# Two matmuls per slice in place of three: x's low and high halves side by side in one 512-column operand, and the two bank halves joined by ScalarE and VectorE

## The chip, the cores and the metric

The kernel runs on one core of a Trainium2 chip. The metric is the device time of one execution in microseconds (us). The kernel before takes 1995.85 us, the median of three runs (1995.22, 1995.85 and 1999.67).

## The reference

Two layers of an encoder trunk work on x of 256 tokens x 2048 channels, all in float32. Each layer does this:

```
h = RMSNorm(x)
u, s5_gate, z, xbc, dt, q, k, v, att_gate, merge_logits = split(h @ w_in)
y_s5  = S5(u) -> GELU -> GLU (a 1024x1024 product) -> * silu(s5_gate)
y_ssd = Mamba-2 SSD(z, xbc, dt), then a gated RMSNorm
y_att = sliding-window attention(q, k, v) * silu(att_gate)
merged = sum over the three branches of sigmoid(merge_logits_b) * (y_b @ w_branch_b)
x = x + merged @ w_out
```

Nearly all arithmetic is in the four weight products: `h @ w_in` (2048 x 11,792 columns), the GLU, the three branch products and `merged @ w_out` (2048 x 2048).

## The kernel before

**Exact products from two halves.** Weights arrive from DRAM as a stream of 1 MB slices (`raw`, 128 x 2048 float32, four buffers). ScalarE rounds a slice to its high part (`hi`, line 683, writes `w_hi`), VectorE subtracts to get the low part (`lo`, line 971, writes `w_lo` over `raw`), and TensorE forms three products: high weights with low x, low weights with high x, and high with high. x has the same two parts, `h_hi` and `h_lo`.

**Two shapes of slice.** A *feature-major* slice ("pair", line 1565) holds 128 output features for all 2048 inputs. The weights are the stationary operand, and the 256 tokens stream. For each of 16 steps k, `prod3` issues three matmuls of 256 columns into one half of a PSUM bank, 48 matmuls in all. A *token-major* slice ("block", line 1590) holds 512 output features; x is stationary, and 512 columns of weights stream.

**The stages of a layer**, with the numbers of slices:
- *Front*: 16 slices. n = 0 to 3 are B and C of the SSD, 4 and 5 are k, 6 and 7 are v (written out, not a pair), 8 to 15 are u. Between them VectorE and ScalarE run long chains of small operations (S5 parameters, dt, convolutions, the norm of k), and TensorE has a few small products that wait for them: `k_ss` (line 1667), `k_rot` (line 1677).
- *Inner*: a loop of 4 x 8 feature-major slices, with one S5 tile in each turn: TensorE's `kv` after slice 1 (lines 1692 and 1698), `cs` after slice 5 (lines 1708 and 1714), VectorE's S5 work at slices 2, 3 and 4.
- *Gates*: a loop of 4 x 12 token-major slices, with S5, SSD and attention tiles.
- *Side gate and GLU*: 8 feature-major slices, then 4 GLU slices ("units", two products of 256 columns side by side).
- *Branches*: 24 token-major slices. *Out*: 16 feature-major slices; x_new = product + x_old.

**What sets the order.** Every engine runs its own instruction list in order, written out by hand; semaphores couple them. `pair_done` counts finished slices. TensorE uses two banks of `mm` in turn, so slice n waits until the result of slice n-2 has been read. VectorE reads each result (`tt_(..., bank, rstd, mult)`, lines 1163 to 1176, 1309, 1459) and then does `lo` for slice n+3. ScalarE does `hi` for slice n+3 as soon as its data has landed; nothing in this list waits for TensorE. SyncE loads slice j+4 once slice j is finished; in the side-gate stage its list also holds two loads of `gin` that wait for VectorE's `ssd_w3` (line 452), and the load of the next weights stands behind them.

Of the kernel before, what the change touches and what calls it, by code (L numbers as in the profile page):

```python
# [15 lines left out]
P = 128  # L16
# [19 lines left out]
N_SG, N_GLU, N_BR, N_OUT, N_LAYER = 96, 104, 108, 132, 148  # L36
BRANCHES = (1, 2, 0)
# [100 lines left out]
def program(nc, x, norm_w, params, consts, bdense, stream, xs_out, order):  # L138

    with ExitStack() as ctx:  # L140
# [23 lines left out]
        h_hi = sb("h_hi", [P, KT, TOK], F32R)  # L164
        h_lo = sb("h_lo", [P, KT, TOK], F32R)
# [40 lines left out]
        ta = sb("ta", [P, TOK])  # L206
        kcur = sb("kcur", [P, TOK])
        vcur = sb("vcur", [P, 2, 64])
        gt = sb("gt", [P, 2, WIDE])
        tA = sb("tA", [P, TOK])  # L210
# [69 lines left out]
        in_read = sem("in_read")  # L280
        gate_sum = sem("gate_sum")
# [391 lines left out]
        def _(e):  # L673
# [19 lines left out]

            def inv_sqrt(S_, name, out, logs, v, wait):
# [12 lines left out]
            with e.Fori(0, DEPTH) as L:  # L707
# [8 lines left out]
                nb = start(L, 0)  # L716
                for n in range(16):
                    hi(nb, n + LEAD)
# [53 lines left out]
                with e.Fori(0, 4) as I:  # L772
                    nb = start(L, N_IN, I, 8)
                    W.s5(L, I, 0)
                    for s in range(8):
                        hi(nb, s + LEAD)
# [127 lines left out]

                for n in range(12):
                    hi(nb, n + LEAD)
# [58 lines left out]
        def _(e):  # L965
# [29 lines left out]
            S_A = {LV: LA, MV: MA}  # L995

# [8 lines left out]
            with e.Fori(0, DEPTH) as L:  # L1005
# [152 lines left out]
                nb = e.snap(L * N_LAYER)  # L1158
                for n in range(16):
# [3 lines left out]
                    e.wait_ge(pair_done, nb + (n + 3))  # L1163
                    bank = mm[:, n % 2, 0:256]
                    if n < 4:
                        LV.mark(tt_(proj[:, BC + n, :], bank, rstd[:], ALU.mult), f"in{n}")
                    elif n < 6:
                        LV.mark(tt_(kt[:, n - 4, :], bank, rstd[:], ALU.mult), "k_raw" if n == 5 else "in4")
# [4 lines left out]
                    elif 8 <= n < 14:  # L1173
                        LV.mark(tt_(by_lag(proj[:, U + n - 8, :]), by_chunk(bank), by_chunk(rstd[:]), ALU.mult), f"in{n}")
                    elif n >= 14:
                        tt_(by_lag(proj[:, U + n - 8, :]), by_chunk(bank), by_chunk(rstd[:]), ALU.mult).then_inc(in_read, 1)
# [126 lines left out]
                with e.Fori(0, 4) as I:  # L1303
                    nb = e.snap(L * N_LAYER + N_IN + I * 8)
                    W.s5(L, I, 0)
# [738 lines left out]
```

## Time and profile before

| | |
|---|---|
| median of 3 runs | 1995.85 us |
| the profiled execution | 1993.25 us, of which the span is 1991.5 us |
| mean granted TensorE clock | 0.99 |
| TensorE busy | 96% of the span |
| VectorE busy | 66% |
| ScalarE busy | 48% |
| GpSimd busy | 27% |
| DRAM traffic | 188 GB/s over the span |

The span is the stretch from the first to the last instruction of the profiled execution. A group of instructions is told by its line in the kernel. Matmuls overlap in the records (each is shown with its way through the array), so the time that one takes from the next is read from the distance of their starts, not from their durations.

### The profile page before, as it was taken

How to read it: one execution, taken by the hardware profiler on the slowest of the kernel's cores; microseconds unless marked ns; L12 is line 12 of the kernel's file. 1: busy time of each engine (PE TensorE's matmuls, PEld its weight loads, DVE VectorE, ACT ScalarE, POOL GpSimd, SP SyncE). 2: the span in 40 equal slices, each digit the busy share in tenths (PEclk: the TensorE clock that was granted, in tenths of full speed). 3: DMA queues.
4: the chain of work that ended last, by engine and by line, in shares of the span. 5: the costliest groups of instructions: out<-in, count | busy, mean ns of one | idle time of the engine just before them, and what ended most of it. 6: DMA issues, size and time to landing. Idle time of an engine off the chain costs nothing.

```text
span 1991.5 us, 38600 instructions
## 1 busy us (share of the span) xinstructions
PE 1911.2 (96%) x13680; PEld 1704.9 (86%) x13680; DVE 1311.9 (66%) x1729; ACT 946.8 (48%) x1160; POOL 530.2 (27%) x578
## 2 busy tenths in 40 slices
PE   4998999999999999999979799999999999999998
PEld 4898999877777798889978799997777778988898
DVE  6855666687776757665567556667776766576654
ACT  5233333566656645333343333336656665543333
POOL 4105444262442000002411254452442410000033
PEclk9998999999999999999989999999999999999999
DMA  6345555555454456665544545555554554566656
GB/s 256 141 154 201 182 181 183 178 182 177 168 177 158 158 180 233 243 233 200 202 155 145 196 165 182 183 187 175 175 170 164 174 171 169 177 244 236 233 194 206
DMA packets 79442, 372.78 MB, mean 187 GB/s; under 512 B 20560, under 2 KB 27216, under 8 KB 40528
## 3 DMA queue, kind: packets, MB, share of 16 engines
q1 hardware_dynamic: 76560, 359.99, 51.8%
q0 software_dynamic: 1088, 6.80, 0.8%
q10 hardware_dynamic: 1696, 4.72, 0.6%
q8 instruction: 58, 0.95, 0.2%
q14 instruction: 40, 0.33, 0.0%
HBM read 351.80 MB, written 21.76 MB: 188 GB/s over the span
## 4 chain that ended last, share of the span: by engine, by line
PE 83%; DVE 6%; issue 4%; DMA 2%; ACT 2%; POOL 1%; SPq 1%; DVEq 0%; ACTq 0%; POOLq 0%
PE mm L1602 13%; PE mm L1604 13%; PE mm L1603 13%; PE mm L1561 11%; PE mm L1562 11%; PE mm L1563 11%; DMA raw<-in_stream 2%; DVE w_lo L974 1%; ACT w_hi L687 1%; PE b L1698 1%; PE by L1762 1%; PE bs L1708 1%; PE b L1753 1%; PE bs L1714 1%; PE b L1774 1%
## 5 line engine op out<-in xcount | busy, mean ns | idle before, releaser
L687 ACT ACTIVATE w_hi<-raw 128x2048 fp32r<-128x2048 f32 x299 | 571.4, 1911 | 696.0 <-DMA raw<-in_stream 685.0
L974 DVE TENSOR_TENSOR w_lo<-raw,w_hi 128x2048 fp32r<-128x2048 f32 x299 | 690.4, 2309 | 245.7 <-ACT w_hi L687 236.8
L1561 PE MATMUL mm<-h_lo,w_hi 128*128 128x256 f32 x2240 | 644.5, 288 | 37.6 <-DVE h_lo L978 37.3
L1562 PE MATMUL mm<-h_hi,w_lo 128*128 128x256 f32 x2240 | 637.4, 285 | 0.0
L1563 PE MATMUL mm<-h_hi,w_hi 128*128 128x256 f32 x2240 | 637.2, 284 | 0.0
L1561 PEld LDWEIGHTS mm<-h_lo,w_hi 128*128 128x128 f32 x2240 | 433.9, 194 | 42.1 <-DVE h_lo L978 37.5
L1562 PEld LDWEIGHTS mm<-h_hi,w_lo 128*128 128x128 f32 x2240 | 433.8, 194 | 1.5 <-issue 1.0
L1563 PEld LDWEIGHTS mm<-h_hi,w_hi 128*128 128x128 f32 x2240 | 433.5, 194 | 0.0
L1602 PE MATMUL mm<-w_lo,h_hi 128*128 128x512 f32 x768 | 317.2, 413 | 0.0
L1604 PE MATMUL mm<-w_hi,h_lo 128*128 128x512 f32 x768 | 301.1, 392 | 0.0
L1603 PE MATMUL mm<-w_hi,h_hi 128*128 128x512 f32 x768 | 299.8, 390 | 0.0
L668 POOL TENSOR_TENSOR ssum<-ssum,proj 128x256 f32<-128x256 f32 x32 | 76.3, 2384 | 388.4 <-ACT proj L960 388.4
L1602 PEld LDWEIGHTS mm<-w_lo,h_hi 128*128 128x128 f32 x768 | 144.2, 188 | 38.2 <-issue 9.4
L1604 PEld LDWEIGHTS mm<-w_hi,h_lo 128*128 128x128 f32 x768 | 144.1, 188 | 32.1
L1603 PEld LDWEIGHTS mm<-w_hi,h_hi 128*128 128x128 f32 x768 | 144.5, 188 | 27.2
L1602 PE MATMUL mm<-w_lo,ys 128*128 128x512 f32 x384 | 150.2, 391 | 5.6 <-DVE acc L1512 5.6
L1604 PE MATMUL mm<-w_hi,ys 128*128 128x512 f32 x384 | 149.5, 389 | 0.0
L1603 PE MATMUL mm<-w_hi,ys 128*128 128x512 f32 x384 | 149.4, 389 | 0.0
L978 DVE TENSOR_TENSOR proj<-mm,rstd 128x256 f32 (+1 forms) x104 | 47.1, 453 | 142.5 <-PE mm L1563 142.1
L538 POOL TENSOR_TENSOR bw<-bd,lam 128x512 f32<-128x512 f32 x16 | 21.5, 1346 | 279.9 <-DMA lam<-lscr 279.9
L1602 PEld LDWEIGHTS mm<-w_lo,ys 128*128 128x128 f32 x384 | 72.1, 188 | 21.1 <-DVE acc L1512 6.5
L1604 PEld LDWEIGHTS mm<-w_hi,ys 128*128 128x128 f32 x384 | 72.1, 188 | 15.1
(309 smaller groups left out, 2319.5 us busy)
## 6 DMA issues: line engine op xcount, KB each, us to landing
raw<-in_stream SPq DMA_DIRECT2D x300, 1024.0 KB, 4.8
gscr<-gt SPq DMA_DIRECT2D x48, 256.0 KB, 6.0
gin<-gscr SPq DMA_DIRECT2D x24, 512.0 KB, 5.6
bd<-in_bdense SPq DMA_DIRECT2D x16, 384.0 KB, 5.2
lam<-lscr SPq DMA_DIRECT2D x128, 32.0 KB, 2.7
x_old<-out POOLq DMA_DIRECT2D x2, 2048.0 KB, 9.7
out<-proj ACTq DMA_DIRECT2D x8, 512.0 KB, 6.3
proj<-in_x SPq DMA_DIRECT2D x4, 512.0 KB, 8.3
```

The source lines that it names most:

```text
L538: SGp.mark(e.tensor_tensor(bw[:], b2, both(lam[:, 0, :]), ALU.mult), "bw0")
L668: e.tensor_tensor(ssum[:], ssum[:], proj[:, bass.ds(I * 4 + (16 + j), 1), :].rearrange("p a b -> p (a b)"), ALU.add).then_inc(x_sum, 1)
L687: e.activation(w_hi[:, j % RAW, :], raw[:, j % RAW, :], ACT.Copy).then_inc(hi_done, 1)
L974: e.tensor_tensor(w_lo[:, j % RAW, :], raw[:, j % RAW, :], w_hi[:, j % RAW, :].bitcast(F32), ALU.subtract).then_inc(lo_done, 1)
L978: return e.tensor_tensor(out, a, b, op)
L1561: e.matmul(out, whi, xlo, start=start, stop=False)
L1562: e.matmul(out, wlo, xhi, start=False, stop=False)
L1563: return e.matmul(out, whi, xhi, start=False, stop=stop)
L1602: e.matmul(mm[:, tok, :], xhi[:, rows], w_lo[:, j % RAW, w], start=first and k == 0, stop=False)
L1603: e.matmul(mm[:, tok, :], xhi[:, rows], w_hi[:, j % RAW, w], start=False, stop=False)
L1604: ins = e.matmul(mm[:, tok, :], xlo[:, rows], w_hi[:, j % RAW, w], start=False, stop=last and k == QUAD - 1)
L1698: ins = e.matmul(b4[rows, r * 256 + j * CH:r * 256 + j * CH + CH], bw[rows, r, j * 64:j * 64 + 64], ut[rows, j, :], start=True, stop=True)
```

## The change

The parts of x move into one tensor `h_both` of [128, 16, 2, 256]: for each k the low part and the high part lie side by side, 512 columns. `pair` now issues two matmuls for each k: the high weights over all 512 columns, into the whole bank (left half: high x low, right half: high x high), and the low weights over the 256 columns of the high part, into the right half. The result is the sum of the two halves. One engine operation reads one half of a bank here, so the sum takes two more operations per slice:

- In the front, inner and side-gate stages ScalarE copies the left half to SBUF (`part`: waits for the slice and for the join before it, since there is one buffer `ta`, in the side gate `t5`), *ahead of* `hi` for slice n+3 in its list. VectorE adds the copy and the right half (`join`), waits for its own result, and multiplies by `rstd` as before.
- In the out stage VectorE adds x_old and the left half, waits, and adds the right half (`x_part`).

The v slices (n = 6, 7), the product for dt, GLU, gates and branches keep their instructions. Their x operands are views of `h_both`.

```diff
-        h_hi = sb("h_hi", [P, KT, TOK], F32R)
-        h_lo = sb("h_lo", [P, KT, TOK], F32R)
+        h_both = sb("h_both", [P, KT, 2, TOK], F32R)
+        h_lo, h_hi = h_both[:, :, 0, :], h_both[:, :, 1, :]
...
+            def part(n, done, count, half=ta):
+
+                e.wait_ge(pair_done, done)
+                e.wait_ge(joined, count)
+                W.settle()
+                e.activation(half[:], mm[:, n % 2, 0:256], ACT.Copy).then_inc(lo_part, 1)
...
                 for n in range(16):
+                    if n not in (6, 7):
+                        part(n, nb[0] + (n + 3), nj + (n if n < 6 else n - 2))
                     hi(nb, n + LEAD)
...
                     for s in range(8):
+                        part(s, nb[0] + (s + 3), nj + s)
                         hi(nb, s + LEAD)
...
                 for n in range(12):
+                    if n < 8:
+                        part(n, nb[0] + (n + 3), nj + n, t5)
                     hi(nb, n + LEAD)
...
+            def join(out, n, count, order=lambda a: a, half=ta):
+
+                e.wait_ge(lo_part, count)
+                W.settle()
+                tt_(out, order(half[:]), order(mm[:, n % 2, 256:512]), ALU.add).then_inc(joined, 1)
+                e.wait_ge(joined, count + 1)
+                W.settle()
...
                     for s in range(8):
-                        e.wait_ge(pair_done, nb + (s + 3))
-                        tt_(flat(proj[:, bass.ds(I * 8 + (16 + s), 1), :]), mm[:, s % 2, 0:256], rstd[:], ALU.mult).then_inc(in_read, 1)
+                        to = flat(proj[:, bass.ds(I * 8 + (16 + s), 1), :])
+                        join(to, s, nj + (s + 1))
+                        tt_(to, to, rstd[:], ALU.mult).then_inc(in_read, 1)
...
-                        tt_(x_tile, mm[:, j % 2, 0:256], flat(x_old[:, bass.ds(I * 4 + j, 1), :]), ALU.add).then_inc(x_new, 1)
+                        tt_(x_tile, mm[:, j % 2, 0:256], flat(x_old[:, bass.ds(I * 4 + j, 1), :]), ALU.add).then_inc(x_part, 1)
+                        e.wait_ge(x_part, e.snap(L * 16 + I * 4 + (j + 1)))
+                        W.settle()
+                        tt_(x_tile, x_tile, mm[:, j % 2, 256:512], ALU.add).then_inc(x_new, 1)
...
-                    ins = prod3(mm[:, j % 2, 0:256], w_hi[:, j % RAW, w], w_lo[:, j % RAW, w], h_hi[:, k, :], h_lo[:, k, :],
-                                k == 0, k == KT - 1)
+                    e.matmul(mm[:, j % 2, :], w_hi[:, j % RAW, w], h_both[:, k].rearrange("p a t -> p (a t)"), start=k == 0, stop=False)
+                    ins = e.matmul(mm[:, j % 2, 256:512], w_lo[:, j % RAW, w], h_hi[:, k, :], start=False, stop=k == KT - 1)
```

On VectorE, slice 3 of a turn of the inner loop, from the read of the result to the end of the scan, before:

```order
L978 ISA [waits pair_done]
L978 TENSOR_TENSOR proj<-mm,rstd 128x256
L973 REGISTER_ALU
L974 TENSOR_TENSOR w_lo<-raw,w_hi 128x2048 [waits hi_done]
L347 REGISTER_ALU
L978 TENSOR_TENSOR prod<-prod,prod_73 128x256 [waits vec_s5]
L978 TENSOR_TENSOR prod<-prod,prod_73 128x256
```

and in the changed kernel (`ta` is ScalarE's copy):

```order
L999 ISA [waits lo_part]
L999 TENSOR_TENSOR proj<-ta,mm 128x256
L1023 REGISTER_ALU
L999 TENSOR_TENSOR proj<-proj,rstd 128x256 [waits joined]
L994 REGISTER_ALU
L995 TENSOR_TENSOR w_lo<-raw,w_hi 128x2048 [waits hi_done]
L351 REGISTER_ALU
L999 TENSOR_TENSOR prod<-prod,prod_72 128x256 [waits vec_s5]
L999 TENSOR_TENSOR prod<-prod,prod_72 128x256
```

VectorE waits for ScalarE instead of TensorE, and does one operation more, which its own next one waits for.

On ScalarE, in the front stage around n = 8 and 9 (`bt` is the tanh of a convolution, `kk` the logarithm and the exponential for the norm of k), before:

```order
L744 ACTIVATE bt<-kk 128x256 [waits vec_layer]
L687 ACTIVATE w_hi<-raw 128x2048 [waits landed3]
L347 REGISTER_ALU
L697 ACT_TABLE_LOAD
L697 ACTIVATE kk<-kk 128x512 [waits vec_layer]
L347 REGISTER_ALU
L699 ACT_TABLE_LOAD
L699 ACTIVATE kk<-kk 128x512 [waits act_layer]
L686 REGISTER_ALU
L687 ACTIVATE w_hi<-raw 128x2048 [waits landed0]
```

and in the changed kernel:

```order
L760 ACTIVATE bt<-kk 128x256 [waits vec_layer]
L702 REGISTER_ALU
L703 REGISTER_ALU [waits pair_done]
L705 ACTIVATE ta<-mm 128x256 [waits joined]
L691 ACTIVATE w_hi<-raw 128x2048 [waits landed3]
L351 REGISTER_ALU
L710 ACT_TABLE_LOAD
L710 ACTIVATE kk<-kk 128x512 [waits vec_layer]
L351 REGISTER_ALU
L712 ACT_TABLE_LOAD
L712 ACTIVATE kk<-kk 128x512 [waits act_layer]
```

The copy of slice 8 stands between the tanh and `hi` for slice 11, and `hi` now stands behind a wait for TensorE and for VectorE's join of the slice before.

## Rows read from the trace of the kernel before

**Rows 1.** The page: span, busy time, and the chain that ended last by engine.
```profile
span 1991.5 us, 38600 instructions
PE 1911.2 (96%) x13680; PEld 1704.9 (86%) x13680; DVE 1311.9 (66%) x1729; ACT 946.8 (48%) x1160; POOL 530.2 (27%) x578
...
PE 83%; DVE 6%; issue 4%; DMA 2%; ACT 2%; POOL 1%; SPq 1%; DVEq 0%; ACTq 0%; POOLq 0%
```
**Rows 2.** Groups: line, engine, operation, out<-in, shape, count | busy us, mean ns.
```profile
L687 ACT ACTIVATE w_hi<-raw 128x2048 fp32r<-128x2048 f32 x299 | 571.4, 1911 | 696.0 <-DMA raw<-in_stream 685.0
L974 DVE TENSOR_TENSOR w_lo<-raw,w_hi 128x2048 fp32r<-128x2048 f32 x299 | 690.4, 2309 | 245.7 <-ACT w_hi L687 236.8
L1561 PE MATMUL mm<-h_lo,w_hi 128*128 128x256 f32 x2240 | 644.5, 288 | 37.6 <-DVE h_lo L978 37.3
```
**Rows 3.** TensorE's waits: for whom, us in total, times, longest.
```profile
PE bs L1692 <- POOL cl L564: 16.6, 2, 8.4
PE b L1667 <- ACT kk L738: 8.1, 2, 4.2
```
**Rows 4.** Timeline (start, us, engine, what), TensorE, 256-column matmuls, 21 apart.
```profile
907.33 0.28 PE L1563 MATMUL mm<-h_hi,w_hi 128*128 128x256 f32 x1
...
909.85 0.28 PE L1563 MATMUL mm<-h_hi,w_hi 128*128 128x256 f32 x1
```
**Rows 5.** Timeline, TensorE, 512-column matmuls, three apart.
```profile
815.07 0.39 PE L1603 MATMUL mm<-w_hi,ys 128*128 128x512 f32 x1
...
815.75 0.39 PE L1603 MATMUL mm<-w_hi,ys 128*128 128x512 f32 x1
```
**Rows 6.** Timeline, TensorE, 256 columns at the low clock, three apart.
```profile
1012.42 0.41 PE L1563 MATMUL mm<-h_hi,w_hi 128*128 128x256 f32 x1
...
1013.06 0.41 PE L1563 MATMUL mm<-h_hi,w_hi 128*128 128x256 f32 x1
```
**Rows 7.** Stretch: length, busy (count) by engine, granted clock, DMA share, GB/s.
```profile
155.00:165.00 10.00, 4.61 (x58) 4.33 (x59) 5.76 (x5) 7.54 (x7) 8.76 (x9) 0.50 0.53 220
```
**Rows 8.** Timeline, VectorE, front stage.
```profile
37.84 0.42 DVE L978 TENSOR_TENSOR sv<-rstd 128x256 f32<-128x256 f32 x1 [2.21 <-ACT rstd L699]
38.29 0.43 DVE L978 TENSOR_TENSOR sv<-sv 128x256 f32<-128x256 f32 x1
...
39.64 0.43 DVE L978 TENSOR_TENSOR proj<-mm,rstd 128x256 f32<-128x256 f32 x1
39.98 2.28 DVE L974 TENSOR_TENSOR w_lo<-raw,w_hi 128x2048 fp32r<-128x2048 f32 x1
```
**Rows 9.** Timeline, ScalarE, front stage.
```profile
74.83 0.42 ACT L744 ACTIVATE bt<-kk 128x256 f32<-128x256 f32 x1 [13.38 <-DVE kk L1138]
75.15 1.90 ACT L687 ACTIVATE w_hi<-raw 128x2048 fp32r<-128x2048 f32 x1
```
**Rows 10.** Timeline, VectorE, slice 4 of the inner loop's second turn.
```profile
231.63 0.42 DVE L978 TENSOR_TENSOR proj<-mm,rstd 128x256 f32 x1 [0.40 <-PE mm L1563]
232.58 2.29 DVE L974 TENSOR_TENSOR w_lo<-raw,w_hi 128x2048 fp32r<-128x2048 f32 x1 [0.53 <-ACT w_hi L687]
...
236.11 0.76 DVE L978 TENSOR_TENSOR state<-state,prod 128x256 f32<-128x256 f32 x2
```
**Rows 11.** Timeline, ScalarE, the same slice.
```profile
230.64 1.91 ACT L687 ACTIVATE w_hi<-raw 128x2048 fp32r<-128x2048 f32 x1 [3.72 <-DMA raw<-in_stream]
```
**Rows 12.** Chain that ended last (start, us, what), the same turn.
```profile
238.37 1.02 PE bs L1714 x64
```
**Rows 13.** Timeline, VectorE, side gate, slice 7.
```profile
748.19 0.42 DVE L978 TENSOR_TENSOR proj<-mm,rstd 128x256 f32<-128x256 f32 x1
```
**Rows 14.** Timeline, SyncE's queue, side gate.
```profile
752.77 1.49 SPq L454 DMA_DIRECT2D gin<-gscr  x2
754.54 10.63 SPq L374 DMA_DIRECT2D raw<-in_stream  x3
```
**Rows 15.** Timeline, ScalarE, GLU: the hyperbolic tangents that slice 11 waits for.
```profile
763.86 0.82 ACT L928 ACTIVATE tg<-mm,bgh 128x256 f32<-128x256 f32 x2
```

More of the change, by code:

```diff
@@ L36 @@
 N_SG, N_GLU, N_BR, N_OUT, N_LAYER = 96, 104, 108, 132, 148
+N_JOIN = 54
 BRANCHES = (1, 2, 0)
@@ L209, in program @@
         gt = sb("gt", [P, 2, WIDE])
+        ta = sb("ta", [P, TOK])
         tA = sb("tA", [P, TOK])
@@ L280, in program @@
         in_read = sem("in_read")
+        lo_part = sem("lo_part")
+        joined = sem("joined")
+        x_part = sem("x_part")
         gate_sum = sem("gate_sum")
@@ L1162, in _ @@
                         W.settle()
-                    e.wait_ge(pair_done, nb + (n + 3))
-                    bank = mm[:, n % 2, 0:256]
+                    if n in (6, 7):
+                        e.wait_ge(pair_done, nb + (n + 3))
                     if n < 4:
-                        LV.mark(tt_(proj[:, BC + n, :], bank, rstd[:], ALU.mult), f"in{n}")
+                        to = proj[:, BC + n, :]
+                        join(to, n, nj + (n + 1))
+                        LV.mark(tt_(to, to, rstd[:], ALU.mult), f"in{n}")
                     elif n < 6:
-                        LV.mark(tt_(kt[:, n - 4, :], bank, rstd[:], ALU.mult), "k_raw" if n == 5 else "in4")
+                        to = kt[:, n - 4, :]
+                        join(to, n, nj + (n + 1))
+                        LV.mark(tt_(to, to, rstd[:], ALU.mult), "k_raw" if n == 5 else "in4")
                     elif n == 7:
@@ L1172, in _ @@
                         LV.mark(ins, "v_in")
[L1173 to L1176, printed above, removed]
+                    elif n >= 8:
+                        to = by_lag(proj[:, U + n - 8, :])
+                        join(to, n, nj + (n - 1), by_chunk)
+                        ins = tt_(to, to, by_chunk(rstd[:]), ALU.mult)
+                        if n < 14:
+                            LV.mark(ins, f"in{n}")
+                        else:
+                            ins.then_inc(in_read, 1)
                     if n == 4:
@@ L1457, in _ @@
                     if n < 8:
-                        e.wait_ge(pair_done, nb + (n + 3))
-                        LV.mark(tt_(proj[:, SG + n, :], mm[:, n % 2, 0:256], rstd[:], ALU.mult), "sg_out" if n == 7 else f"sg{n}")
+                        join(proj[:, SG + n, :], n, nj + (n + 1), half=t5)
+                        LV.mark(tt_(proj[:, SG + n, :], proj[:, SG + n, :], rstd[:], ALU.mult), "sg_out" if n == 7 else f"sg{n}")
                     else:
```

8 lines of the change are left out of this document (7 added, 1 removed).

## The prediction

> **What bounds the kernel now.** I read the page first: TensorE is busy for 96% of the span and holds 83% of the chain that ended last; VectorE and ScalarE are at 66% and 48% [rows 1]. Then TensorE's waits, which tell where it does not set the pace: 16.6 us ahead of the first S5 product of each layer, 8.1 us ahead of `k_ss`, both in or just behind the front stage [rows 3], where VectorE's and ScalarE's lists are one long dependent chain. Everywhere else the starts of the matmuls follow one another without a gap worth a row, save at the layers' ends and once in each branch stage. So a saving on TensorE counts in the inner, side-gate and out stages; a delay on VectorE or ScalarE counts in the front.
>
> **What a slice costs TensorE.** The durations of 288 ns [rows 2] overlap, so I take distances of starts. 21 narrow matmuls lie in 909.85 - 907.33 = 2.52 us, 0.120 us each [rows 4]; three wide ones in 0.68 us, 0.227 us each [rows 5]. The streaming itself at 2.4 GHz is 0.107 and 0.213 us, so either width carries about 0.0135 us besides, once for each matmul with its own weights. A step k now takes 3 x 0.120 = 0.360 us, and then 0.227 + 0.120 = 0.347 us. The columns streamed stay the same (768), and one fixed part goes. With 16 steps a slice falls from 5.76 to 5.55 us, by 0.21 us. That is all that the change can give: 3.6% of such slices, though a third of their instructions goes.
>
> At the low clock nothing goes: there a narrow matmul takes 0.64 / 3 = 0.213 us [rows 6], which is 256 columns at 1.2 GHz with no fixed part left, and 512 + 256 columns cost what 3 x 256 cost. After TensorE's wait of 8.4 us at the first S5 product the granted clock is 0.50 [rows 3, 7], so about one slice per layer behind it saves nothing.
>
> Slices that count, per layer: 29 of the inner stage (30 stand behind the S5 wait), 8 side gate, 16 out: 53. Two layers: 106 x 0.205 = 21.7 us. (The front's slices are in the next part. 70 slices x 16 steps x 2 layers = 2240, the count of [rows 2].)
>
> The Trainium skill speaks against even this. "TensorE: Matmul & The Clock Gate", section "Back-to-back issue gap", puts the gap between matmuls at full clock at columns / 2.4 plus 2.5 ns. By that a step would save 2.5 ns, and the 106 slices 4.2 us. The trace has 13.5 ns beside the streaming at both widths (rows 4 and 5), with a weight load in front of each matmul, and I follow it; the page's number stands as a rival below.
>
> **The front stage, per layer.** VectorE is the chain here. A 256-wide operation that the next one waits for occupies it for 38.29 - 37.84 = 0.45 us, one that nothing waits for 39.98 - 39.64 = 0.34 us [rows 8]. `join` adds one of the former. ScalarE's copy is a 256-wide operation ahead of another one: 75.15 - 74.83 = 0.32 us [rows 9].
> - Joins 0 to 4 stand on the chain to the first convolution: 5 x 0.45 = 2.25 us. TensorE has finished these slices long before VectorE comes to them, so the copies are ready, and only the add counts.
> - At n = 5, 8 and 9 ScalarE is on the chain (tanh, or log and exp, then `hi`, then `lo`). The copy stands ahead of `hi`: 3 x 0.32 = 1.0 us. The joins of these slices hide under VectorE's wait for that `hi`, 1.91 us long [rows 2].
> - Join 10 stands behind `kn`, and slice 12 needs its result: 0.45 us.
> - Slices 0, 12 and 13 are shorter: 3 x 0.2 = -0.6 us.
> Sum: +3.1 us at the point at which SyncE starts the DMAs that the first S5 product waits for. From there GpSimd's chain has fixed lengths, and TensorE idles anyway (8.4 us, then more), so all of it arrives: +3.1 us per layer. Bounds: 1.5 us, if half of the adds fall into waits; 8 us, if every one of the 14 copy-and-join hand-overs adds its 0.32 + 0.45 on the path. I take 3.1. The waits at `k_ss` and the S5 product grow by some 3 us and 1 us; they are idle time at a place that is late already, and a longer stretch at the low clock falls before the next wait, or costs up to 2 us.
>
> **The inner stage.** In slice 4 VectorE reads the result at 231.63, starts `lo` 0.95 us later, and ends the S5 states at 236.87, 5.24 us after the read [rows 10]. `hi` was running by 230.64, before the slice had ended [rows 11]. Now ScalarE's list reaches `hi` only after the slice has ended and the copy has gone, so `hi` starts at 0.35 us, ends at 2.27 us, and `lo` starts at 2.3 us, 1.35 us later than now. The join (copy 0.42, add 0.45, multiply 0.34) fits in under that. The states then end 6.59 us after the read. The matmuls that need them start at 238.37, 6.74 us after it [rows 12], and by 0.2 us earlier with a shorter slice: 6.53 us. So the slack of 1.5 us is used up, and I charge 0.15 us x 8 turns = 1.2 us (bounds 0 and 4 us). VectorE starts slices 3 and 4 about 1 us late, but `hi` decides when `lo` begins, so the lateness does not grow. The banks are free 1.5 to 2.3 us after a slice, against 5.55 us; w_lo is ready 4.5 us after a slice and wanted 11 us after it. Neither stops TensorE.
>
> **Side gate.** The same 1.35 us and more falls on slices 6 and 7, where VectorE has the gated norm. It reads slice 7 at 748.19 [rows 13], at once when it is finished, and will come to it some 2.3 us late; `ssd_w3` then lands 1.1 us after slice 8 ends (that is 748.05 + 5.8 = 753.85) instead of 1 us before it. SyncE's list has the two `gin` loads behind that wait, and the weights for slice 12 behind those: 752.77 and 754.54 now [rows 14], and 2.1 us later against TensorE's course. ScalarE's `hi` for that slice and the tangents behind it end at 763.86 + 0.82 = 764.7 [rows 15]; slice 11 needs them at 753.85 + 2 x 5.8 = 765.4. The slack of 0.7 to 0.9 us turns into a stall of 1.3 us per layer (0 to 3). Behind it everything hangs on the end of slice 11, as now.
>
> **Out stage.** One add in front of x_new. VectorE has some 4 us of work in a slice of 5.55 us (three short operations and a `lo` of 2.31 us [rows 2]), so only the last slice of a layer shows it: 0.45 us per layer.
>
> **Sum.** Costs 2 x (3.1 + 1.3 + 0.45) + 1.2 = 10.9 us, saving 21.7 us: -10.8 us. The profiled execution took 1993.25 us, which would become 1982.4. The median of the runs is 2.6 us above that execution, so I forecast 1985 us.
>
> **Rivals.**
> 1. *More comes through*: the costs are at their low bounds (2 x 1.5 for the front, nothing in the side gate or the inner loop, 0.9 at the ends): 21.7 - 3.9 = 17.8 us saved, 1978 us. For it: most of what is added lies on engines that are idle for a third of the time or more. Against: these stages are chains. 0.12.
> 2. *The chains eat it*: the front costs 8 us per layer, the inner loop 4 us: 16 + 4 + 2.6 + 0.9 = 23.5 against 21.7, +1.8 us, 1998 us; with the front at 6 us, 1994. For it: ScalarE and VectorE now wait for each other in every slice (a copy for the join before it, a join for the copy, `hi` behind the copy). Against: in most front slices TensorE and ScalarE are ahead of VectorE. 0.13, most of it within 0.2%.
> 3. *The fixed part does not go* (slower): TensorE takes the 512 and the 256 columns of a step in 0.360 us, because the weights for the next matmul come no sooner when wide and narrow ones alternate. Nothing is saved, all costs stay: +10.9 us, 2007 us. It decides at one number, the distance from one high-weight matmul to the next: with 0.353 us the saving equals the costs. For it: no row shows the two widths in turn; before a narrow and before a wide matmul the load is seen only with neighbours of the same width. Against: both widths carry the same fixed part. 0.10.
> 4. *The rule of the page* (slower): the saving is 4.2 us, +6.7 us, 2002.5 us. 0.05.
>
> My forecast has the remaining 0.60. A change of 0.2%, 4 us, is about what a measurement of this kernel can tell from none. Faster by more than that: 0.60 + 0.12, less a few in which the costs reach 18 us: 0.70. Slower: rivals 3 and 4 and the upper end of 2: 0.17. Same: 0.13. The range from 1976 to 2000 leaves out the far ends of rivals 1, 3 and 4. The forecast's own range is 1979 to 1991.
>
> **What would show it.** Starts of the high-weight matmuls 0.347 us apart, and 5.55 us per slice, show the saving; 0.360 shows rival 3. The first S5 product of a layer should start about 3 us later after the layer's start; TensorE's waits for the S5 states (now line 1714) should be small or none; there should be a wait of 1 to 2 us at the last GLU slice, and ScalarE's `hi` in the inner loop should start right behind the copy. A front that grows by over 6 us, or TensorE stalls in most turns of the inner loop, would make the forecast wrong.

## The result, and the profile after

The kernel with the change takes 2018.8 us (median, 2013.7 to 2023.7); the kernel before, timed beside it, takes 1996.1 us. The ratio is 1.0105, with a 95% interval of 1.0077 to 1.0133. The change makes the kernel slower by about 1%. The forecast was 1985 us, and its range ended at 2000 us: both the sign and the range were wrong.

The page of the profiled execution answers to [rows 1] and [rows 2]. Groups are line, engine, operation, out<-in, shape, count | busy us, mean ns | idle before, releaser.

```profile
span 2018.8 us, 35039 instructions
...
PE 1908.1 (95%) x11440; PEld 1592.2 (79%) x11440; DVE 1383.2 (69%) x1869; ACT 979.7 (49%) x1268; POOL 526.4 (26%) x578
...
PE 78%; DVE 8%; issue 5%; ACT 3%; DMA 3%; POOL 1%; SPq 1%; DVEq 0%; ACTq 0%; POOLq 0%
...
L1617 PE MATMUL mm<-h_both,w_hi 128*128 128x512 f32 x2240 | 812.1, 406 | 43.6 <-DVE h_both L999 35.4
...
L1618 PE MATMUL mm<-h_both,w_lo 128*128 128x256 f32 x2240 | 634.4, 283 | 0.0
```

2240 matmuls with their weight loads have gone, and yet the span is 27.3 us longer. TensorE's share of the chain fell from 83% to 78%, and VectorE's rose from 6% to 8%. TensorE's busy time is no measure here, since the durations overlap. The waits tell more. These are the seven longest of TensorE's waits (for whom: us in total, times, longest), which answer to [rows 3]:

```profile
PE mm L1617 <- DVE h_both L999: 35.4, 2, 26.4
PE bs L1736 <- POOL cl L568: 19.0, 2, 9.7
PE bs L1758 <- DVE state L999: 17.4, 8, 2.6
PE b L1711 <- ACT kk L754: 13.2, 2, 6.8
PE mm L1617 <- DVE proj L999: 7.9, 9, 2.1
PE mm L1646 <- DVE acc L1553: 5.8, 2, 2.9
PE mm L1605 <- ACT tg L949: 3.4, 2, 1.9
```

The third line is the new one: TensorE waits in each of the eight turns of the inner loop for the S5 states, 17.4 us in all. Before, this wait did not exist. The fourth grew from 8.1 to 13.2 us; the fifth and the last (the tangents for the last GLU slice) are new as well.

To see where the time went I read the start of the same matmul in both traces at the borders of the stages: the sum of squares in a layer's front, the first S5 product of the first turn, the first S5 product behind the inner loop, the last gate head, the first transposition of the branch stage. The differences to the kernel before, both layers added up, in us (the kernels beside the change come below; the last mark is the start of the last matmul, so a sum can differ from the difference of the spans by up to 1 us):

| stage | forecast | the change | GpSimd waits | no join | inner and out only | two wide, two narrow |
|---|---|---|---|---|---|---|
| up to the first sum of squares | 0 | -0.6 | -1.1 | -1.4 | -0.3 | +0.2 |
| front | +6.2 | +11.4 | +11.3 | +4.2 | +0.7 | +2.2 |
| inner loop | -10.7 | +16.6 | -5.5 | -5.5 | -5.3 | -8.7 |
| gate heads | 0 | +1.2 | +0.4 | +0.2 | +2.7 | +2.4 |
| side gate and GLU | -0.7 | +4.3 | +3.8 | -3.1 | +3.5 | +1.8 |
| branch and out | -5.7 | -5.2 | -4.1 | -2.4 | -5.2 | -7.2 |
| sum | -10.9 | +27.7 | +4.8 | -7.9 | -3.9 | -9.4 |

Of the 39 us between the two sums, 27 lie in the inner loop. A front that no edit touches is itself not the same in every trace: in the last column, where the front is the old one, its second layer is 3.1 us longer, because TensorE's wait ahead of `k_rot` was followed there by 8 us at a mean granted clock of 0.57.

**The inner loop.** Timeline of VectorE in the second turn (start, us, what, [idle before <- releaser]), which answers to [rows 10]:

```profile
237.44 0.39 DVE L999 TENSOR_TENSOR proj<-ta,mm 128x256 f32 x1
...
238.82 2.29 DVE L995 TENSOR_TENSOR w_lo<-raw,w_hi 128x2048 fp32r<-128x2048 f32 x1 [0.41 <-ACT w_hi L691]
241.03 0.68 DVE L999 TENSOR_TENSOR state<-prod,tab 128x512 f32<-128x512 f32 x1
241.63 1.76 DVE L999 TENSOR_TENSOR prod<-prod,tab 128x512 f32<-128x512 f32 x1
243.43 2.23 DVE L999 TENSOR_TENSOR state<-state,prod 128x256 f32<-128x256 f32 x2
```

Timeline of ScalarE, the same slice (for [rows 11]):

```profile
236.60 0.39 ACT L705 ACTIVATE ta<-mm 128x256 f32<-128x256 f32 x1 [3.37 <-PE mm L1618]
236.88 1.91 ACT L691 ACTIVATE w_hi<-raw 128x2048 fp32r<-128x2048 f32 x1
```

Timeline of GpSimd, the same time:

```profile
241.56 1.28 POOL L542 TENSOR_TENSOR bw<-bd,lam 128x512 f32<-128x512 f32 x1 [18.24 <-DMA lam<-lscr]
242.92 1.59 POOL L544 TENSOR_TENSOR bd<-bd,lam 128x512 f32<-128x512 f32 x1
...
245.34 0.91 POOL L547 TENSOR_TENSOR bw<-bw,bd 128x256 f32<-128x256 f32 x1
```

The lateness of `lo` is what the prediction said: the copy starts when the slice ends, `hi` right behind it, and `lo` 2.22 us after the copy's start (2.3 forecast). The end is not. The product at 241.03, which began while GpSimd was still idle, takes 0.68 us; the one at 241.63, of the same shape, takes 1.76 us, and the pair of 256-wide state operations takes 2.23 us where [rows 10] have 0.76 us. These three operations run beside GpSimd's S5 products, which a DMA (`lam`) releases 4.96 us after the slice has ended, in this turn of both kernels. Before, the states were done at 236.87 and GpSimd began at 236.59; now VectorE comes later and runs into it. The states end 9.1 us after the copy began, where 6.59 was forecast and 6.53 the limit. TensorE waits the difference, and starts again at the low clock (timeline, then the stretch behind it, which has 0.66 of the clock; columns as in [rows 7]):

```profile
245.71 1.91 PE L1758 MATMUL bs<-state,cz 128*32 128x63 f32 x64 [2.51 <-DVE state L999]
247.55 0.80 PE L1617 MATMUL mm<-h_both,w_hi 128*128 128x512 f32 x1
248.14 0.42 PE L1618 MATMUL mm<-h_both,w_lo 128*128 128x256 f32 x1
248.36 0.63 PE L1617 MATMUL mm<-h_both,w_hi 128*128 128x512 f32 x1
```

```profile
245.00:250.00 5.00, 4.29 (x74) 3.80 (x75) 3.77 (x4) 1.91 (x1) 4.69 (x5) 0.66 0.39 164
```

The Trainium skill, "GPSIMD Engine Reference", section "Specifications", says that GpSimd's access to SBUF is shared with VectorE, and that they contend when VectorE has two inputs in SBUF. The trace agrees: the product and the state operations read two SBUF tiles each, and the product takes 2.6 times as long (1.76 against 0.68 us).

**The step.** Timeline of TensorE's wide matmuls in the out stage, 21 steps apart, at full clock, of the changed kernel (for [rows 4]):

```profile
931.88 0.40 PE L1617 MATMUL mm<-h_both,w_hi 128*128 128x512 f32 x1
...
939.30 0.40 PE L1617 MATMUL mm<-h_both,w_hi 128*128 128x512 f32 x1
```

7.42 / 21 = 0.353 us, where the forecast had 0.347 and three narrow ones take 0.360. A finer look shows two levels: over any stretch in which TensorE does nothing else, the step is either 0.3467 or 0.3533 us, and it keeps that level until a wait or another kind of matmul comes. In the changed kernel about half of such stretches are at 0.3467, but they are the shorter ones: counted by steps it is a third (some 650 of 2050), and both out stages are at 0.3533. So a mean slice saves 0.14 us and not 0.21 us (16 steps, 0.107 us at one level and 0.213 us at the other).

### The profile page after: what moved, and what is told of

Same layout as the page of the kernel before. It is cut to its first block, busy times and chain, and to the rows that moved or that the text cites. A ratio compares the mean times of both kernels' runs of the same rounds, so it can differ in the third digit from the quotient of the medians.

```text
span 2018.8 us, 35039 instructions
## 1 busy us (share of the span) xinstructions
PE 1908.1 (95%) x11440; PEld 1592.2 (79%) x11440; DVE 1383.2 (69%) x1869; ACT 979.7 (49%) x1268; POOL 526.4 (26%) x578
## 4 chain that ended last, share of the span: by engine, by line
PE 78%; DVE 8%; issue 5%; ACT 3%; DMA 3%; POOL 1%; SPq 1%; DVEq 0%; ACTq 0%; POOLq 0%
PE mm L1617 20%; PE mm L1646 13%; PE mm L1648 13%; PE mm L1647 13%; PE mm L1618 10%; ACT w_hi L691 2%; DVE w_lo L995 2%; DMA raw<-in_stream 1%; PE b L1742 1%; PE by L1806 1%; PE bs L1758 1%; DMA uscr<-proj 1%; PE b L1797 1%; DVE state L999 1%; PE b L1818 1%
## 5 line engine op out<-in xcount | busy, mean ns | idle before, releaser
L1617 PE MATMUL mm<-h_both,w_hi 128*128 128x512 f32 x2240 | 812.1, 406 | 43.6 <-DVE h_both L999 35.4
L1618 PE MATMUL mm<-h_both,w_lo 128*128 128x256 f32 x2240 | 634.4, 283 | 0.0
L1617 PEld LDWEIGHTS mm<-h_both,w_hi 128*128 128x128 f32 x2240 | 428.7, 191 | 153.3 <-DVE h_both L999 35.7
L1618 PEld LDWEIGHTS mm<-h_both,w_lo 128*128 128x128 f32 x2240 | 430.9, 192 | 1.6 <-issue 1.3
L1646 PE MATMUL mm<-w_lo,h_both 128*128 128x512 f32 x768 | 317.3, 413 | 0.0
L1648 PE MATMUL mm<-w_hi,h_both 128*128 128x512 f32 x768 | 301.1, 392 | 0.0
L1647 PE MATMUL mm<-w_hi,h_both 128*128 128x512 f32 x768 | 299.8, 390 | 0.0
L1646 PEld LDWEIGHTS mm<-w_lo,h_both 128*128 128x128 f32 x768 | 144.2, 188 | 38.2 <-issue 9.4
L1648 PEld LDWEIGHTS mm<-w_hi,h_both 128*128 128x128 f32 x768 | 144.1, 188 | 32.1
L1647 PEld LDWEIGHTS mm<-w_hi,h_both 128*128 128x128 f32 x768 | 144.5, 188 | 27.2
L999 DVE TENSOR_TENSOR proj<-ta,mm 128x256 f32 (+1 forms) x88 | 39.9, 453 | 106.3 <-ACT ta L705 104.1
L1648 PEld LDWEIGHTS mm<-w_hi,ys 128*128 128x128 f32 x384 | 72.7, 189 | 15.3
L1647 PEld LDWEIGHTS mm<-w_hi,ys 128*128 128x128 f32 x384 | 72.9, 190 | 14.9
```

The source lines that it names most:

```text
L999: return e.tensor_tensor(out, a, b, op)
L1617: e.matmul(mm[:, j % 2, :], w_hi[:, j % RAW, w], h_both[:, k].rearrange("p a t -> p (a t)"), start=k == 0, stop=False)
L1618: ins = e.matmul(mm[:, j % 2, 256:512], w_lo[:, j % RAW, w], h_hi[:, k, :], start=False, stop=k == KT - 1)
L1646: e.matmul(mm[:, tok, :], xhi[:, rows], w_lo[:, j % RAW, w], start=first and k == 0, stop=False)
L1647: e.matmul(mm[:, tok, :], xhi[:, rows], w_hi[:, j % RAW, w], start=False, stop=False)
L1648: ins = e.matmul(mm[:, tok, :], xlo[:, rows], w_hi[:, j % RAW, w], start=False, stop=last and k == QUAD - 1)
```

## The experiments

Each ratio is against the kernel before on the same chip, with its 95% interval. Medians of the kernel before were 1996.4 us in the first group of four, 1994.4 in the second, 1994.6 in the third, 1993.7 us in the last two.

**Only the matmuls back to three.** Copy, join and second add stay; the step is three narrow matmuls, the first into the left half, the others into the right.

```
-  matmul(mm[:, j % 2, :],       w_hi, h_both[:, k])
-  matmul(mm[:, j % 2, 256:512], w_lo, h_hi)
+  matmul(mm[:, j % 2, 0:256],   w_hi, h_lo)
+  matmul(mm[:, j % 2, 256:512], w_lo, h_hi)
+  matmul(mm[:, j % 2, 256:512], w_hi, h_hi)
```

> The whole reading side of the change (copy, join, out-stage add) with three matmuls of 256 columns per step again: low x into the left half of the bank, the other two into the right. Theory: the reading side costs all that was lost and the two-matmul step gives a little back. The step of the changed kernel is 0.353 us (199.62 to 199.97) against 0.360, so 0.11 us a slice or about 12 us in all; this kernel should then be slower than the changed one by 8 to 12 us, some 2026 us, with waits of TensorE for the S5 states near 2 us each, as there. Rival, the wide matmul itself (its 512-column reads of x, or the changed layout) disturbs the others: this kernel is back near 1996 to 2005 us, and the S5 states take 2.1 us again.

Measured: 2036.6 us, ratio 1.0206 [1.0189, 1.0223], 10 us more than expected. The step is 0.360 us everywhere in the trace. So the two-matmul step gives 2036.6 - 2018.8 = 18 us, and the reading side costs 40 us. Added up over the changed kernel's trace, its steps at full clock fall short of 0.360 us by 18.3 us, of which the 106 slices of the prediction have 14.4 and the front 3.9. Rival 3, by which nothing is saved, is out. TensorE waits 19.3 us for the states here too, so it is not the wide matmul that brings this wait.

**No join.** VectorE multiplies the right half alone, as it multiplied the one sum before; the product of the high weights and the low half of x is computed and left out of the result.

```
-  join(to, s, nj + (s + 1))
-  tt_(to, to, rstd[:], ALU.mult)
+  tt_(to, mm[:, s % 2, 256:512], rstd[:], ALU.mult)
```

> The two-matmul step alone: VectorE multiplies the right half of the bank as the kernel before multiplied its result, nothing reads the left half (so the product of high weights and low x is left out), no copy, no join, no second add. Theory: TensorE sets the pace as before, 106 slices save 0.11 us each: -12 us, 1982 to 1987 us. By the step I forecast, 0.347 us, it would be -22 us, 1974. Rival, wide and narrow in turn save nothing: 1996.

Measured: 1987.3 us, ratio 0.9962 [0.9951, 0.9972]. TensorE's waits in this kernel, behind the one for `h_both`:

```profile
PE bs L1722 <- POOL cl L568: 17.6, 2, 8.9
PE b L1697 <- ACT kk L750: 9.6, 2, 4.9
PE b L1707 <- DVE kk L1245: 6.0, 2, 3.6
```

The wait for the states is gone, and the kernel is 9 us faster than before, not 21.7. That is less than the 18 us of the experiment above, and the table says where the rest is: the front is 4.2 us longer. `k_ss` and `k_rot` start at the same place in the layer as before (within 0.1 us), so it isn't the reading side. Behind TensorE's wait ahead of `k_rot` the clock fell in both layers (mean 0.57 over 114 to 118 us and 0.52 over 1094 to 1101 us, where the kernel before has 1.00 behind a wait of 2.8 and 1.8 us), as it did in the one layer named above. How often it does so is not known from one trace of each kernel, so the 9 us stand for what was measured and not for a limit.

**GpSimd waits.** The changed kernel, and GpSimd begins its S5 products only when VectorE has formed the state.

```
   W.wait(SP, "KV", 1)
+  W.wait(SV, "sim", 1)
   tensor_tensor(bw[:], b2, ...)
```

> The changed kernel with one wait more: GpSimd starts its four products for the next S5 tile (line 542) only when VectorE has written the S5 states of this one. Theory: in the inner loop VectorE's last products (two SBUF inputs each) now fall into GpSimd's, where they take 1.76 and 2.23 us in place of 0.69 and 0.76; with the two kept apart they take the short times again, TensorE's waits for the states fall from 2.2 us to under 0.3 us, the drops of the clock behind them go too, and 12 to 22 us come back: 1997 to 2007 us. Rival, VectorE is late by its place in the order alone: the products take their short times but the kernel stays within 5 us of the changed one, 2014 or more.

Measured: 1997.2 us, ratio 1.0004 [0.9994, 1.0013]: 22 us less than the changed kernel, and the table has the inner loop at -5.5 instead of +16.6. VectorE (groups by shape, 160 to 350 us: count | busy us, mean ns | idle), first of the changed kernel, then of this one:

```profile
L999 DVE TENSOR_TENSOR state<-state,prod 128x256 f32<-128x256 f32 x8 | 8.5, 1104 | 0.1
L999 DVE TENSOR_TENSOR prod<-prod,tab 128x512 f32<-128x512 f32 x4 | 6.0, 1492 | 0.0
```

```profile
L1000 DVE TENSOR_TENSOR state<-state,prod 128x256 f32<-128x256 f32 x8 | 3.0, 422 | 0.1
L1000 DVE TENSOR_TENSOR prod<-prod,tab 128x512 f32<-128x512 f32 x4 | 2.7, 685 | 0.0
```

TensorE has no wait for the states any more, though every copy and join is still there. So the 22 us are contention and what follows from it: 17.4 us of waits, and more time at the low clock behind them (mean granted clock of the inner loop 0.97 instead of 0.99), not the length of VectorE's list.

**The same wait in the kernel before**, as a control:

> The kernel before with GpSimd's wait alone (its S5 products begin only when VectorE has formed its state). Control for the 21.6 us that this wait gave the changed kernel. Theory (GpSimd and VectorE slow each other only where their products overlap, and before they overlap hardly at all): 1995 to 1998 us, no difference. Rival (the wait is good by itself, by the order it gives GpSimd, whatever the reading side): 1980 us or less. Second rival (GpSimd's work is late by it and TensorE waits): above 2000 us.

Measured: 1993.8 us, ratio 0.9995 [0.9984, 1.0006]. The wait is worth nothing by itself. But the durations of the state operations (same groups, 175 to 350 us) are worth a look; first the kernel before, then the control:

```profile
L978 DVE TENSOR_TENSOR state<-state,prod 128x256 f32<-128x256 f32 x8 | 5.2, 693 | 0.1
```

```profile
L979 DVE TENSOR_TENSOR state<-state,prod 128x256 f32<-128x256 f32 x8 | 3.0, 422 | 0.1
```

The state operations already met GpSimd in the kernel before (693 ns instead of 422). The mean hides how: in six of the eight turns of the inner loop the second state operation took 1.50 us, and only in the first two turns of the first layer 0.42 us. [rows 10] are the second of these two. The third turn, VectorE, GpSimd and TensorE (the last line is cut at the window's end):

```profile
281.69 0.42 DVE L978 TENSOR_TENSOR proj<-mm,rstd 128x256 f32 x1 [0.59 <-PE mm L1563]
...
286.30 1.84 DVE L978 TENSOR_TENSOR state<-state,prod 128x256 f32<-128x256 f32 x2
```

```profile
286.51 1.35 POOL L538 TENSOR_TENSOR bw<-bd,lam 128x512 f32<-128x512 f32 x1 [20.00 <-DMA lam<-lscr]
```

```profile
288.36 0.65 PE L1714 MATMUL bs<-state,cz 128*32 128x63 f32 x32
```

The states are done 6.45 us after the read and TensorE wants them 6.67 us after it. The slack is 0.2 us in this turn and 0.1 to 0.3 us in all six, where the prediction had 1.5 us.

**High halves first.** In the slices around the states (2, 3, 4) ScalarE rounds before it copies, and VectorE forms `lo` before the join.

```
-  part(s, ...); hi(nb, s + LEAD)        # ScalarE
+  hi(nb, s + LEAD); part(s, ...)
-  join(to, s, ...); ...; lo(nb, s + LEAD)   # VectorE
+  lo(nb, s + LEAD); join(to, s, ...); ...
```

> The changed kernel with another order at slices 2, 3 and 4 of the inner loop: ScalarE rounds the weights before it copies the bank half, VectorE subtracts before it joins. Theory: VectorE no longer waits for a rounding that starts behind the end of the slice, is 1.3 us earlier at the states, and most of them are done before GpSimd starts: waits of TensorE for the states from 2.2 to about 0.5 us, 10 to 18 us back, 2001 to 2009 us. Rival, the order costs nothing and only the two added operations count: within 4 us of the changed kernel.

Measured: 2012.1 us, ratio 1.0085 [1.0068, 1.0101]. The medians differ by 7 us, not the 10 to 18 expected, and the intervals of the two ratios overlap, so the times alone do not show the gain. The traces do: the inner loop is at +7.2 us instead of +16.6, and TensorE waits 11.9 us in six turns instead of 17.4 in eight. The product is faster (955 ns), but the state operations still take 1108 ns. Another order on VectorE moves only a part of the overlap.

**Low weights into the left half.** Is the slower level of the step due to the narrow matmul adding to the columns just written?

```
-  matmul(mm[:, j % 2, 256:512], w_lo, h_hi)
+  matmul(mm[:, j % 2, 0:256],   w_lo, h_hi)
```

> The changed kernel with GpSimd's wait (1997.2 us), and one more edit: the narrow matmul (low weights by the high half of x) adds into the left half of the bank instead of the right one. The sum of the halves stays the same. In the right half the narrow matmul adds to the columns that the wide one has written last, in the left half to those that it wrote first. Theory A: this order inside the bank is why a step takes 0.353 us and not 0.347: then the step falls to 0.347 and the time by about 106 slices x 16 x 0.006 = 10 us, to 1987 us. Theory B: the wide matmul's 0.235 us in place of 0.227 comes from widths in turn or from elsewhere: no change of the step, 1996 to 1998 us.

Measured: 1999.7 us, ratio 1.0022 [1.0009, 1.0035]. The time is 2 us above the range of theory B. Most steps are at 0.3533 us, the whole second out stage among them, and both levels occur, as without the edit. Theory A falls.

**Inner and out stages only.** Front and side gate have three matmuls and the one read again, GpSimd waits.

```
   with e.Fori(0, 4) as I: ... pair(nb, s)
-  pair(nb, n)                   # front, side gate
+  pair(nb, n, three=True)       # as before, no part, no join
```

> Front and side gate with the three narrow matmuls and the single read of before, the two-matmul step with copy and join in the inner and out stages only, with GpSimd's wait. By the stages of the traces: the front's +3.4 us and the side gate's +2 us per layer go, the inner stage keeps its saving (-4.4 us and -1.6 to -4.4 us), the out stage its -2.3 us per layer: 1982 to 1987 us. Rival (front and inner stage depend on each other, and what the front no longer loses is lost again at the wait ahead of the first S5 product or elsewhere): 1990 us or more.

Measured: 1986.8 us, ratio 0.9963 [0.9949, 0.9977]. The front is back to +0.7 us. Against the changed kernel with GpSimd's wait (1.0004) that is 8 us. At the first gate slices a new wait of 1.1 us per layer takes part of the inner loop's saving (gate heads +2.7 us).

**Out stage only.**

> Two-matmul step in the out stage alone, where VectorE adds both halves to x itself and nothing is copied; all else reads and multiplies as before, no wait on GpSimd. By the step of 0.353 us: 32 slices x 0.11 = 3.5 us saved, less 0.45 us at the end of each layer: 1993.7 us. By the stage marks of the changed kernel's trace (3.4 and 1.6 us): 1991.4 us. Rival (the out stage's gain belongs to the earlier stages' delay, which is caught up there): 1996 us.

Measured: 1990.6 us, ratio 0.9977 [0.9967, 0.9987]. By the stage marks -4.0 us at the end of the first layer and -1.7 us at the end of the second. The wide matmuls of the first out stage, 21 steps apart:

```profile
931.76 0.40 PE L1611 MATMUL mm<-h_both,w_hi 128*128 128x512 f32 x1
...
939.04 0.39 PE L1611 MATMUL mm<-h_both,w_hi 128*128 128x512 f32 x1
```

7.28 / 21 = 0.3467 us here and 0.3533 in the second layer: 256 steps x 0.0067 = 1.7 us between the layers, from the level alone. The rest of the difference lies at the border of the layers, where TensorE's wait is 9.6 us instead of 11.1.

**Inner and out stages only, without GpSimd's wait.**

> The two-matmul step in the inner and out stages, the front and the side gate as before, and GpSimd without its wait. Theory (copy and join inside the inner loop alone make VectorE late enough to overlap GpSimd's S5 products; the front's delay has no part in it): VectorE's product takes about 1.5 us and the states about 1.1 us each, TensorE waits 2 us in each of the 8 turns: 1987 + 17 to 21 = 2004 to 2008 us. Rival (the overlap came from the front's delay, which shifted VectorE against GpSimd): the durations of the kernel before, 1985 to 1990 us.

Measured: 2008.6 us, ratio 1.0071 [1.0058, 1.0084], 22 us more than with the wait. TensorE's wait and VectorE's groups (175 to 350 us):

```profile
PE bs L1753 <- DVE state L995: 20.5, 8, 2.6
```

```profile
L995 DVE TENSOR_TENSOR state<-state,prod 128x256 f32<-128x256 f32 x8 | 8.9, 1154 | 0.1
L995 DVE TENSOR_TENSOR prod<-prod,tab 128x512 f32<-128x512 f32 x4 | 7.1, 1767 | 0.0
```

So the copy and join inside the loop bring the overlap by themselves; the front's delay is not needed for it. It is the second pair of kernels that differ in that wait alone, with the same answer.

**The front alone as before** (side gate with the new step, GpSimd waits):

> The changed kernel with GpSimd's wait, and the front alone back at three narrow matmuls and the single read; the side gate keeps the two-matmul step with its copy and join. Separates the two prices. Theory, from stage marks: the side gate's wait for the last GLU slice comes back (2 us per layer, less 0.9 us saved on its 8 slices, less the 1.2 us lost at the first gate slice): 1988 to 1991 us, and TensorE waits about 2 us per layer for the tangents. Rival (the stall of the side gate was brought by the front's delay): 1985 to 1987 us.

Measured: 1988.8 us, ratio 0.9971 [0.996, 0.9983]. The front's stages are at +0.1 and 0.0 us, where the table has 11.3 us for the kernel with GpSimd's wait. In the whole time 6.6 us come back (1.0004 to 0.9971), less than that, and 2 us of the rest are the new wait at the first gate slices. The stall of the side gate is there without the front's delay. TensorE's waits of this kernel:

```profile
PE b L1709 <- ACT kk L753: 8.1, 2, 4.2
...
PE mm L1599 <- ACT tg L948: 3.2, 2, 1.8
```

**High halves first, once more**, on the kernel with inner and out stages only and GpSimd's wait:

> The two-matmul step in the inner and out stages with GpSimd's wait (1986.8 us), and in slices 2, 3 and 4 of a turn ScalarE rounds the weights before it copies, VectorE forms their low half before it joins. With no contention left, TensorE has no stall in the inner loop, so the order should be worth nothing: 1985 to 1988 us. Rival (the order was worth its 7 us in the changed kernel by itself, not by moving VectorE away from GpSimd): 1980 us.

Measured: 1986.0 us, ratio 0.9954 [0.9941, 0.9967], which is not told apart from 0.9963. Without contention the order is worth nothing that can be measured, so what it gave in the changed kernel fits with VectorE being moved against GpSimd.

**Two wide, then two narrow.** The same kernel, with the matmuls of two steps regrouped.

```
-  for k: wide(k); narrow(k)
+  for k in steps of 2: wide(k); wide(k + 1); narrow(k); narrow(k + 1)
```

> The two-matmul step in the inner and out stages with GpSimd's wait (1986.8 us, ratio 0.9963), with the matmuls of two steps in another order: two wide ones, then the two narrow ones. Same products, half as many changes of width. The traces show the step at two levels, 0.3467 us and 0.3533 us, each kept over a stretch without an interruption; this kernel's trace has all stretches of the inner and out stages at the upper one. Theory A (a change of width costs): a step falls to 0.3467 us everywhere, 2 x 46 slices x 16 x 0.0066 = 9.7 us less, 1977 us. Theory B (the level is set by where in time a stretch starts, not by the order of widths): 1982 to 1989 us, with both levels or the upper one in the trace.

Measured: 1981.7 us, ratio 0.9935 [0.9921, 0.9949], against 0.9963 without. Pairs of wide matmuls in the first out stage, 12 pairs apart:

```profile
931.98 0.63 PE L1614 MATMUL mm<-h_both,w_hi 128*128 128x512 f32 x2
...
940.34 0.63 PE L1614 MATMUL mm<-h_both,w_hi 128*128 128x512 f32 x2
```

8.36 / 24 = 0.3483 us, in both layers and in all stretches but for some 0.0003 us. The order of widths matters, but theory A's 0.3467 is not reached.

**Groups of four.**

> The kernel with two wide, then two narrow matmuls (1981.7 us, step 0.3484 us), with groups of four instead of two in the inner and out stages. Read from the trace: the step. Theory A (a change of width costs a small fixed time, and without one wide and narrow keep their 0.227 and 0.120 us): alternating 0.3533, groups of two 0.3484, so groups of four about 0.347 to 0.3475 us, and 0 to 2 us less in all. Theory B (the step settles at levels that no count of width changes explains): 0.3484 us or more, no change of the time.

Measured: 1984.4 us, ratio 0.9952 [0.9937, 0.9966]. Four groups of four lie between these rows:

```profile
934.16 1.09 PE L1613 MATMUL mm<-h_both,w_hi 128*128 128x512 f32 x4
...
939.77 1.09 PE L1613 MATMUL mm<-h_both,w_hi 128*128 128x512 f32 x4
```

5.61 / 16 = 0.3506 us: slower than groups of two, with half as many changes of width (the times, 0.9952 and 0.9935, have intervals that overlap; the steps decide). Theory A falls. What sets the level of the step stays open.

**Groups of two, high halves first.**

> The fastest kernel so far (two wide, then two narrow matmuls in the inner and out stages, GpSimd's wait; ratio 0.9935) with ScalarE's rounding ahead of its copy and VectorE's low half ahead of the join in slices 2, 3 and 4. This order alone gave 0.9954 beside 0.9963, which is no difference. Theory: again none, ratio 0.992 to 0.9945, 1979 to 1984 us. Rival (it spares the 1.1 us that TensorE waits at the first gate slice of a layer, and the two add up): ratio 0.991 or less.

Measured: 1978.8 us, ratio 0.9934 [0.992, 0.9948]. No difference to 0.9935; the 1.1 us at the first gate slice of a layer are still there, and the rival falls. The two kernels with groups of two are the fastest measured, 0.65% under the kernel before.

## Why the prediction was wrong, step by step

**The step that failed is the inner loop's.** The prediction worked out when VectorE would form the states from durations in one turn of the trace of before (5.24 us from read to end), moved them by 1.35 us, and found 6.59 us against a limit of 6.53. The move was right: `lo` starts 2.22 us after the copy, 2.3 forecast. Two things were wrong. The first is the row: [rows 10] show one of the two turns in which VectorE does not run beside GpSimd. In the other six the states already took 6.4 to 6.5 us, which with the 1.35 us is an estimated 1.2 to 1.4 us too late, some 8 us in all, where the prediction charged 1.2. The second is that the durations did not move unchanged: 1.35 us later they stand deeper in GpSimd's four products, and in the second turn three operations take 2.5 us longer together. Each turn then costs TensorE up to 2.6 us of waiting and some steps at the low clock. Forecast for both layers: +1.2 us (bounds 0 and 4); the pairs of kernels with and without GpSimd's wait have 22 us. The upper bound left out the mechanism altogether: it bounded lateness by the slack, not the length of the late work. None of the rivals had it either; rival 2, "the chains eat it", came nearest in kind, but stopped at 1998 us. The prediction did name TensorE stalls in most turns of the inner loop as a sign that would make it wrong.

**The saving was mis-sized.** 0.347 us per step is one of two levels that occur, 0.353 the other, and two thirds of the steps are at the latter: 14.4 us instead of 21.7 for the 106 slices, by the sum over the trace. The whole effect measured, 18 us, has the front's slices in it, which the prediction left out of the saving. The fixed part is not one for each matmul, whatever its neighbours: [rows 4] and [rows 5] were rows of equal widths in a row, and alternating ones behave otherwise, as rival 3 said, at the upper level by half of its size. The prediction named 0.353 as the point at which the saving equals the costs; the step came to lie there for two thirds of the steps. The rule of the Trainium skill ("TensorE: Matmul & The Clock Gate", section "Back-to-back issue gap", rival 4, a saving of 4.2 us), which the page gives for an isolated matmul, is not borne out by the 18 us measured.

**The front costs 5.7 us per layer, not 3.1**, in the changed kernel and in the one with GpSimd's wait, in both layers; the bounds were 1.5 and 8. (The upper one does not follow from its own words, 14 times 0.32 + 0.45, which is 10.8.) The mechanism holds, the term is short: `k_ss` is 3.7 us late in both layers of both kernels, and on time in the kernel without copy and join. One piece is the join itself. VectorE in the front of the changed kernel, for [rows 8]:

```profile
39.19 0.42 DVE L999 TENSOR_TENSOR proj<-ta,mm 128x256 f32<-128x256 f32 x1 [0.24 <-DVE rstd L999]
39.77 0.42 DVE L999 TENSOR_TENSOR proj<-proj,rstd 128x256 f32<-128x256 f32 x1 [0.15 <-DVE proj L999]
40.11 2.29 DVE L995 TENSOR_TENSOR w_lo<-raw,w_hi 128x2048 fp32r<-128x2048 f32 x1
```

From add to multiply it is 0.58 us, and the sum had 0.45; up to `k_ss` its terms (five joins and a copy) gave 2.6 us of the 3.7. A second piece may be a transfer: SyncE's longest wait for the DMA of `uscr` grew from 6.2 to 8.1 us, 15.8 instead of 12.0 us in all; but it is 14.4 us in the kernel without copy and join too, so most of this growth is not theirs. Whether the new waits for a free bank (7.9 us, [rows 3] have none) add the rest was not tried.

**The side gate went as written, and a little further.** SyncE's `gin` loads wait for the gated norm (13.0 us instead of 8.5), the weights queue behind them, and the tangents behind those. SyncE's queue and ScalarE, for [rows 14] and [rows 15]:

```profile
766.74 0.82 SPq L458 DMA_DIRECT2D gin<-gscr  x2
767.84 9.02 SPq L378 DMA_DIRECT2D raw<-in_stream  x3
```

```profile
775.47 1.91 ACT L691 ACTIVATE w_hi<-raw 128x2048 fp32r<-128x2048 f32 x1 [6.21 <-DMA raw<-in_stream]
777.29 0.82 ACT L949 ACTIVATE tg<-mm,bgh 128x256 f32<-128x256 f32 x2
```

TensorE waits 3.4 us for them in two layers, 1.9 and 1.5; 1.3 was forecast. The stage as a whole grew by 2.1 us per layer, more than this wait less what its eight slices save (1.3 us). The rest is not settled: in the kernel with inner and out stages only, whose side gate is the old one, the stage still came out 0.2 us longer in one layer and 3.2 us in the other.

**The out stage** came out right in size, -5.7 us forecast and -5.2 measured, but by luck. Its steps are at 0.3533 us in both layers and save 3.4 us, not 6.6. The rest came from the border of the layers, where TensorE's wait fell from 11.1 to 8.9 us and the prediction had put 0.45 us on top.

Put together for the kernel without contention: +4.8 us by its trace against -10.9 forecast, of which the front is 5.1 us, the inner loop's smaller saving 5.2, the side gate and GLU 4.5, and the other stages 0.9 us. So even with the contention away the whole change gains nothing (1.0004); it gains where the reading side is off the path, and that is the inner and out stages.

## What to carry to other kernels

A duration read from a trace belongs to its neighbours in time, and one turn of a loop need not stand for the others: here the turn that was read had 1.4 us of slack and six of eight had 0.1 to 0.3 us. Before moving VectorE work that reads two SBUF tiles, see what GpSimd does at the new place, and compare the duration of the same operation with its shortest in the trace (here 693 against 422 ns). Where two engines contend and one of them has time, a wait on the one that has time can be worth more than any reordering of the other (22 us here, for one line that costs nothing in the kernel before). A change that takes work from the busiest engine and gives it to idle ones is best made stage by stage: the same edit won 0.2% in the out stage and lost 5.7 us per layer in the front.

## What the runs showed of the hardware that was not expected

- A 512 and a 256 column matmul in turn, each with its own weights, take 0.3467 or 0.3533 us together, and a stretch keeps its level. In groups of two they take 0.3483 us, in groups of four 0.3506 us, and three of 256 columns 0.360 us. The cause is open.
- VectorE's 512-wide product took 1.76 us beside GpSimd's and 0.68 us alone; its 256-wide operation 0.94 to 1.50 us beside it against 0.42 us. GpSimd's own product was slowed far less, from 1.36 us (mean, with its wait) to 1.53 us.
- TensorE's wait at the border between the layers fell from 11.1 to 9.6 us in the kernel in which only the out stage was changed, though the last slice's chain has an add more, and it is 8.6 to 9.5 us in the other kernels with the new step and its reading side. A part of this is scatter between executions: the kernel before with GpSimd's wait, whose out stage is the old one, has 10.0 us. The cause of the rest is open.
